# A two-layer diffusion step on one core: latent rows normalised, rotated and turned between the value and the query projections

## What is computed

```python
q_na, k_na, v_na, cq, ckv, k_rope = split(h @ w_in)         # 512, 512, 512, 256, 128, 32 columns
q_mla = (_rms_norm(cq, q_norm_g) @ w_uq).reshape(b, l, 8, 96)
ckv = _rms_norm(ckv, kv_norm_g)
k_rope = _axial_rope(k_rope, rows_pos, cols_pos)             # latent tokens only
kv = (ckv @ w_ukv).reshape(b, l, 8, 128)                     # keys and values of the latent heads
```

## Time and profile before

| | us |
|---|---|
| median of 3 runs | 1071.36 |
| lowest and highest | 1070.34, 1072.72 |
| profiled execution | 1072.17 |
| its span | 1070.3 |
| TensorE busy in it | 984.8 |

### The profile page before, as it was taken

The page is one execution under the profiler, slowest core; times in us unless marked ns, Lnnn a source line. Parts: engine busy times, 40 slices in busy tenths (PEclk is TensorE's granted clock), DMA queues, the critical chain, the costliest instruction groups (busy, mean ns, idle before and its releaser), DMA issues.

```text
span 1070.3 us, 14368 instructions
## 1 busy us (share of the span) xinstructions
PE 984.8 (92%) x5585; PEld 480.2 (45%) x5585; DVE 341.0 (32%) x872; ACT 251.6 (24%) x597; POOL 122.6 (11%) x138
## 2 busy tenths in 40 slices
PE   4899889999899999987889999999989999999896
PEld 3445546555433334432344554566553344343332
DVE  2200376521832122111330025764156112211226
ACT  2110155421411111111320103553041111111113
POOL 4120200000211111110022002000011111111103
PEclk8999999999899999999999999999998999999999
DMA  9952375378489999999995035662955999999993
GB/s 356 390 205 79 111 277 219 125 304 344 164 323 396 396 393 409 393 407 417 386 366 197 20 131 206 237 237 93 419 235 203 377 391 386 395 410 407 410 409 121
DMA packets 64666, 314.21 MB, mean 294 GB/s; under 512 B 7674, under 2 KB 9942, under 8 KB 38736
## 3 DMA queue, kind: packets, MB, share of 16 engines
q1 hardware_dynamic: 56112, 289.06, 69.2%
q0 software_dynamic: 7616, 21.01, 5.6%
q10 hardware_dynamic: 864, 3.15, 0.7%
HBM read 301.06 MB, written 17.53 MB: 298 GB/s over the span
## 4 chain that ended last, share of the span: by engine, by line
PE 71%; DMA 17%; DVE 6%; issue 2%; ACT 2%; SPq 2%; POOL 0%; DVEq 0%; ACTq 0%
PE psum L1066 15%; DMA arena<-in_w_up 12%; PE psum L1456 8%; PE psum L1310 8%; PE psum L1123 7%; DMA arena<-in_w_ada 5%; PE psum L1298 4%; PE psum L1289 3%; PE psum L983 3%; PE psum L1396 3%; PE psum L1426 2%; PE psum L1408 2%; PE psum L1078 2%; PE psum L1351 2%; PE psum L1022 1%
## 5 line engine op out<-in xcount | busy, mean ns | idle before, releaser
L1066 PE MATMUL psum<-arena 128*64 128x512 f32 x512 | 235.6, 608 | 21.7 <-DMA arena<-in_w_up 17.8
L1069 PE MATMUL psum<-arena 128*64 128x512 f32 x512 | 236.1, 609 | 0.0
L1066 PEld LDWEIGHTS psum<-arena 128*64 128x64 f32 x512 | 69.2, 140 | 168.6 <-issue 164.2
L1123 PE MATMUL psum<-arena 128*64 128x512 f32 x512 | 118.7, 600 | 3.3 <-ACT arena L1615 1.4
L2046 DVE SCALAR_TENSOR_TENSOR arena<-arena,psum 64x512 f32<-64x512 f32 (+1 forms) x32 | 23.9, 747 | 259.5 <-ACT arena L1609 259.5
L1456 PE MATMUL psum<-arena 128*128 128x384 f32 x256 | 86.7, 492 | 0.0
L1310 PE MATMUL psum<-arena 128*128 128x384 f32 x256 | 83.5, 487 | 1.2 <-PE psum L1310 0.6
L1609 ACT ACTIVATE arena<-psum 64x512 f32<-64x512 f32 (+1 forms) x32 | 20.6, 644 | 263.6 <-PE psum L1069 263.6
L1069 PEld LDWEIGHTS psum<-arena 128*64 128x64 f32 x512 | 69.2, 140 | 0.0
L1310 PEld LDWEIGHTS psum<-arena 128*128 128x128 f32 x256 | 48.3, 190 | 36.8 <-issue 4.0
L1456 PEld LDWEIGHTS psum<-arena 128*128 128x128 f32 x256 | 47.3, 190 | 32.4 <-issue 2.7
(11 more groups left out here) (305 smaller groups left out, 1216.5 us busy)
## 6 DMA issues: line engine op xcount, KB each, us to landing
arena<-in_w_gate SPq DMA_DIRECT2D x54, 1024.0 KB, 20.9
arena<-in_w_up SPq DMA_DIRECT2D x50, 1024.0 KB, 23.3
arena<-in_w_ada SPq DMA_DIRECT2D x24, 2048.0 KB, 7.8
arena<-in_w_down SPq DMA_DIRECT2D x48, 1024.0 KB, 22.8
arena<-in_w_down SPq DMA_DIRECT2D x32, 512.0 KB, 22.1
arena<-in_w_up SPq DMA_DIRECT2D x28, 512.0 KB, 21.2
arena<-in_w_in SPq DMA_DIRECT2D x6, 2048.0 KB, 14.6
arena<-in_w_gate SPq DMA_DIRECT2D x20, 512.0 KB, 14.5
```

What stands on the lines that cost most here:

```text
L1066: ins = nc.tensor.matmul(bank[b][0:MAIN, :], hg[:, k, 0:MAIN], row(wg[half], k), start=(k == 0), stop=(k == KD - 1))
L1069: ins = nc.tensor.matmul(bank[b][MAIN:P, :], hg[:, k, 0:MAIN], row(wu[half], k), start=(k == 0), stop=(k == KD - 1))
L1123: ins = nc.tensor.matmul(bank[6][MAIN * j:MAIN * j + MAIN, :], hidT[:, c, 0:MAIN], down_row(w[half], c)[:, 512 * j:512 * j + 512], start=( ...
```

## The change

The five groups of transposes that follow the keys are split. CQT, CKVT and KRT are filled between V and QK; KOUT and KC stay behind QK. The items are renumbered so that each keeps its engine: CQT 6 and 7, CKVT 8, KRT 9, QK 10 to 17, KOUT 18, KC 19. The wait for the caches moves from KC to CKVT, since `ckvn` holds cached rows too. ScalarE takes its statistics ahead of its V copy, VectorE its normalising and rotating ahead of its two V copies, and each then copies CQT, CKVT and KRT, then QK, KOUT, KC and QM items. No instruction is added or taken away, and no size changes. POOL's program is the same text, with KRT now coming earlier than KOUT by the whole QK projection.

```diff
--- before.py
+++ after.py
@@ -60,7 +60,7 @@
 ADA_EARLY = 4
 
 
-IT_REST, IT_V, IT_QK, IT_KOUT, IT_KC, IT_CQT, IT_CKVT, IT_KRT = 0, 3, 6, 14, 15, 16, 18, 19
+IT_REST, IT_V, IT_CQT, IT_CKVT, IT_KRT, IT_QK, IT_KOUT, IT_KC = 0, 3, 6, 8, 9, 10, 18, 19
 IT_QM, IT_VM, IT_KM, IT_QMT, ITEMS = 20, 26, 30, 38, 46
 UNITS = 24
 OUT_DMAS = 4
@@ -886,12 +886,16 @@
                     ins.then_inc(item_dve, 1)
 
         def copies_latent(eng, l, parity):
-            copy_out(eng, l, parity, IT_KOUT, IT_KC, lambda i: k_out)
-            copy_out(eng, l, parity, IT_KC, IT_CQT, lambda i: kcT.rearrange("p a b -> p (a b)"))
             copy_out(eng, l, parity, IT_CQT, IT_CKVT, lambda i: cqT[:, i, :], width=TOK,
                      scale=lambda i: vec[:, l, 64 + i:65 + i])
             copy_out(eng, l, parity, IT_CKVT, IT_KRT, lambda i: ckvT)
-            copy_out(eng, l, parity, IT_KRT, IT_QM, lambda i: krT[0:QKD, :], parts=QKD)
+            copy_out(eng, l, parity, IT_KRT, IT_QK, lambda i: krT[0:QKD, :], parts=QKD)
+
+        def copies_keys(eng, l, parity):
+            copy_out(eng, l, parity, IT_KOUT, IT_KC, lambda i: k_out)
+            copy_out(eng, l, parity, IT_KC, IT_QM, lambda i: kcT.rearrange("p a b -> p (a b)"))
+
+        def copies_queries(eng, l, parity):
             copy_out(eng, l, parity, IT_QM, IT_VM, lambda i: qtok[:, i // 2, 512 * (i % 2):512 + 256 * (i % 2)],
                      width=lambda i: 512 - 256 * (i % 2))
 
@@ -1298,7 +1302,23 @@
                         ins = nc.tensor.matmul(bank[(IT_V + t) % 4][:, :], hT[:, k, P * t:P * t + P], w[:, k, :],
                                                start=(k == 0), stop=(k == KD - 1))
                     ins.then_inc(item_ps, 1)
-                release(l, IT_QK)
+                release(l, IT_CQT)
+                pe.wait_ge(lora_norm, l + 1)
+                for i in range(2):
+                    item_free(pe, l, IT_CQT + i)
+                    for t in range(NT):
+                        ins = nc.tensor.transpose(bank[(IT_CQT + i) % 4][:, P * t:P * t + P], cqn[:, t, P * i:P * i + P], ident)
+                    ins.then_inc(item_ps, 1)
+                pe.wait_ge(cache_in, 64 * l + 64)
+                item_free(pe, l, IT_CKVT)
+                for m in range(4):
+                    ins = nc.tensor.transpose(bank[IT_CKVT % 4][:, P * m:P * m + P], ckvn[:, m, :], ident)
+                ins.then_inc(item_ps, 1)
+                pe.wait_ge(kr_ready, l + 1)
+                item_free(pe, l, IT_KRT)
+                for m in range(4):
+                    ins = nc.tensor.transpose(bank[IT_KRT % 4][0:QKD, P * m:P * m + P], kr[:, m, :], ident)
+                ins.then_inc(item_ps, 1)
                 for half in range(2):
                     key = ("q", l) if half == 0 else ("k", l)
                     loaded(key)
@@ -1319,24 +1339,8 @@
                     ins = nc.tensor.transpose(bank[IT_KOUT % 4][:, P * m:P * m + P], qkT[:, 4 + m, 0:P], ident)
                 ins.then_inc(item_ps, 1)
                 item_free(pe, l, IT_KC)
-                pe.wait_ge(cache_in, 64 * l + 64)
                 for m in range(4):
                     ins = nc.tensor.transpose(bank[IT_KC % 4][:, P * m:P * m + P], kc_tok[:, P * m:P * m + P], ident)
-                ins.then_inc(item_ps, 1)
-                pe.wait_ge(lora_norm, l + 1)
-                for i in range(2):
-                    item_free(pe, l, IT_CQT + i)
-                    for t in range(NT):
-                        ins = nc.tensor.transpose(bank[(IT_CQT + i) % 4][:, P * t:P * t + P], cqn[:, t, P * i:P * i + P], ident)
-                    ins.then_inc(item_ps, 1)
-                item_free(pe, l, IT_CKVT)
-                for m in range(4):
-                    ins = nc.tensor.transpose(bank[IT_CKVT % 4][:, P * m:P * m + P], ckvn[:, m, :], ident)
-                ins.then_inc(item_ps, 1)
-                pe.wait_ge(kr_ready, l + 1)
-                item_free(pe, l, IT_KRT)
-                for m in range(4):
-                    ins = nc.tensor.transpose(bank[IT_KRT % 4][0:QKD, P * m:P * m + P], kr[:, m, :], ident)
                 ins.then_inc(item_ps, 1)
                 item_wait(pe, l, IT_CQT)
                 item_wait(pe, l, IT_CQT + 1)
@@ -1672,7 +1676,6 @@
                     copy_rows(0, 0)
                 modulate(l, 0)
                 copy_out(act, l, 0, IT_REST, IT_V, lambda i: rest[:, i, :], width=REST)
-                copy_out(act, l, 0, IT_V, IT_QK, lambda i: vtok[:, i, :])
 
                 for t in range(NT):
                     item_wait(act, l, IT_REST + t)
@@ -1683,9 +1686,12 @@
                 st.sync()
                 nc.scalar.activation(rstat[:, 0:3], stat[:, 0:3], ACT.Sqrt, bias=eps, scale=1.0 / RANK_Q)
                 nc.scalar.activation(rstat[:, 3:6], stat[:, 3:6], ACT.Sqrt, bias=eps, scale=1.0 / RANK_KV).then_inc(lora_stat, 1)
+                copy_out(act, l, 0, IT_V, IT_CQT, lambda i: vtok[:, i, :])
                 load_table(ACT.Exp)
+                copies_latent(act, l, 0)
                 copies_qk(act, l, 0)
-                copies_latent(act, l, 0)
+                copies_keys(act, l, 0)
+                copies_queries(act, l, 0)
                 copies_values(act, l, 0)
                 copies_q(act, l, 0)
                 def exps(u):
@@ -2171,8 +2177,6 @@
                 else:
                     norm(2 * l)
                 copy_out(dve, l, 1, IT_REST, IT_V, lambda i: rest[:, i, :], width=REST)
-                copy_out(dve, l, 1, IT_V, IT_QK, lambda i: vtok[:, i, :])
-                copies_qk(dve, l, 1)
 
                 dve.wait_ge(lora_stat, l + 1)
                 st.did(v.reciprocal(rstat, rstat))
@@ -2190,7 +2194,11 @@
                 rope(kr[:, 3, HD:QKD].unsqueeze(1), 2, 1)
                 st.sync()
                 dve.sem_inc(kr_ready, 1)
+                copy_out(dve, l, 1, IT_V, IT_CQT, lambda i: vtok[:, i, :])
                 copies_latent(dve, l, 1)
+                copies_qk(dve, l, 1)
+                copies_keys(dve, l, 1)
+                copies_queries(dve, l, 1)
                 for t in range(1, NT):
                     item_wait(dve, l, IT_QM + 2 * t)
                     item_wait(dve, l, IT_QM + 2 * t + 1)
```

## The result

The changed kernel takes 1066.29 us in the median of 10 runs (1061.65 to 1068.77), the kernel before 1072.27 (10 runs, 1070.34 to 1075.47). The ratio is 0.9941, with a 95% interval of 0.9927 to 0.9956: 6.3 us less, between 4.7 and 7.8 (the two medians are 6.0 apart). The profiled execution of the changed kernel is its fastest, 1061.65.

What follows compares the result with a forecast made beforehand. TensorE holds 71% of the last-ending chain, DMA 17%, so TensorE's waits count. Gains of 3.11 and 4.85 sum to 7.96 us: 1064.2 from the profiled 1072.17, 1063.4 from the median, taken as 1064.0; range 1062.3 to 1067.8.

Steps and rivals of the forecast that it cites:

- Added ahead of the queries: Between values and queries, the transposes of `cqn`, `ckvn` and `kr` would add 1.66 us a layer to TensorE.
- Removed: Behind the keys, 4.77 us a layer would go: 5.24 between the starts of L1324 and L1351, less a pitch of 0.47.
- Net: In one layer's stretch from values to latent-head queries, 4.77 - 1.66 = 3.11 us gained.
- The clock, and layer 1: Behind layer 1's keys, half speed would vanish, worth 1.74 us, so layer 1 gains 3.11 + 1.74 = 4.85.
- The upper end: During the values, VectorE's normalising chain waits for all of POOL's bias addition and ends at 68.2, still 6.8 us early.
- The cover: Time between the normalising chain's end and the values' end on TensorE: 13.6 us, or 6.8 if POOL's addition holds the chain.
- The banks, the caches, the releases: Around the moved transposes, PSUM bank waits, cache transfers and SP's later release of `w_ada` pieces were taken to cost nothing.
- Passing on: Through the DMA-bound expert stages the gain reaches the end, since expert weights are issued earlier by the same amount.
- the new places: Rival: clock falls anyway at transposes ahead of queries or around the 0.70 us wait; 1066.0 or 1067.7 us; chance 0.16.
- Swallowing: Rival: expert-stage transfers absorb the gain, leaving 1071.4 us; chance 0.08 for all, 0.05 for half.
- The late chain: Rival: normalising ends beyond 78.1, so TensorE stands ahead of the queries; 1074.2 us if at 80 in both layers; chance 0.03.
- The sum: Over both layers, 3.11 + 4.85 = 7.96 us gained, giving a forecast of 1064.0 us.

Runs made afterwards that it cites:

- before_again: The kernel before, unchanged, profiled and timed again against itself: median 1072.47 us, ratio 0.9986 (0.9963 to 1.0009).
- single-layer kernels: The kernel before with VectorE's query and key copies put behind its normalising and rotating, in layer 0 alone or layer 1 alone: ratios 0.9952 and 0.9953.
- the two repeats: The changed kernel, unaltered, timed twice more against the kernel before: medians 1065.43 and 1065.86 us, ratios 0.9920 and 0.9924.
- after_again: The changed kernel, unaltered, run again beside the kernel before: median 1065.43 us, ratio 0.9920 (0.9893 to 0.9946).
- chain_behind_values: The changed kernel with value copies back ahead of ScalarE's statistics and VectorE's normalising chain: median 1073.84 us, ratio 1.0004 to the kernel before.

## Why the prediction was right, and where it was off

- *The terms of one layer.* Added ahead of the queries: 1.66 forecast, 1.56 measured. Removed: 4.77 forecast; 5.24 - 0.43 = 4.81 measured, and QM itself takes 8.21 from start to start instead of 8.29. From the first query product to KOUT it is 42.68 instead of 42.75. Net 3.40 in layer 0 against 3.11.
- *The clock, and layer 1.* 4.85 was forecast for layer 1 and 5.14 measured, but the split was wrong: the gaps were forecast at 3.11 and are worth 2.98, the fall at 1.74 and cost 2.15. The prediction gave layer 1 the gaps of layer 0 and took the difference of the two stretches, 58.49 - 56.75 = 1.74, for the price of half speed. The three other profiles of the kernel before have layer 1 without a fall, at 56.33 or 56.34. So its gaps alone are worth 56.34 - 53.36 = 2.98, 0.42 less than the 3.40 of layer 0, and the fall in it cost 58.49 - 56.34 = 2.15. The difference of 1.74 held both at once, which is why the sum does not show the error. The shorter gap comes from VectorE: in layer 0 of each of the four profiles it stands still for 0.56 us ahead of the rotations (L1855), in layer 1 it does not, and L1339 waits 1.44 instead of 1.85. The first line is layer 0 in the profile before, the second layer 1 of before_again:

```profile
120.24 0.40 DVE L1855 TENSOR_TENSOR arena<-arena 128x8 f32<-128x8 f32 x4 [0.56 <-DVE arena L2184]
645.91 0.61 PE L1339 MATMUL psum<-arena 128*96 128x128 f32 x4 [1.44 <-DVE arena L883]
```

  Why layer 0 has this pause is not shown. The step also took the fall for a feature of layer 1. It belongs to either layer, one of them in each profile of the kernel before, so the sum holds for an average execution; that one fall was the usual number, and not none or two, could not be known from one profile and is luck.
- *The chain under POOL's addition.* The upper end came true: 67.14, forecast 68.2 at most. What was held was a copy with one input, not the instructions with two that the prediction named (last section). The cover, 7.5 us in layer 0, sufficed.
- *The banks, the caches, the releases* cost nothing, as taken: no wait stands at CQT, CKVT, KRT or the first query group but the 0.30 that was there before.
- *Passing on.* Shown by the single-layer kernels and by the constant length of what follows. The first expert weights were issued at 216.32; 217 had been forecast.
- *The rivals.* No fall came in the new places. Swallowing is refuted. The late chain is real as a mechanism, at 4.08 us a layer when the cover is taken away, but does not arise.
- *The sum.* 7.96 us forecast. By the traces the two stretches together went from 115.0 to 115.2 down to 106.7, 8.2 to 8.5 us. The first timed comparison gave 6.3 (4.7 to 7.8), the two repeats 8.6 and 8.1. The local sum lies within the intervals of the repeats and just outside the first. The medians are closer together, 6.0, 6.9 and 7.3 us apart, all below the local sum. And beside the same runs that gave the 8.6, the unchanged kernel came out at 0.9986, 1.5 us less than itself, so part of the 8.6 may be scatter. The timed runs put the gain between 6 and 8.6 us; the forecast of 1064.0 was 2.3 us below the first median, 1066.29. Whether the local sum reaches the end whole is not settled, and what the first set lacks, up to 2 us, is not explained. Other falls of the clock move such a sum: at the REST projection one came in 6 of 8 layers of the profiles of the kernel before and in 4 of 6 of the changed one, at 1.5 to 1.7 us each, and the profiled execution of 1061.65 has none. Why they come in one execution and not in another stays open.

## What to carry to other kernels

When the engine on the critical path waits for a short chain of small operations elsewhere, see when the inputs of that chain were ready. Here they had been ready for 46 us and the chain stood behind copies in its own queue; moving one line of that queue gave as much as the whole rearrangement. A pause in a thin stretch of TensorE may cost more than its own length, so price it at both clock levels, and look at several profiles before putting a fall down to one place.

## What was not expected of the hardware

A VectorE copy of 32 columns, 0.17 to 0.18 us in the kernel before, was recorded with 6.69 us when POOL's addition had begun 0.01 us earlier. Layer 1 of the same profile, first in VectorE's timeline, then in POOL's:

```profile
572.26 4.67 DVE L2186 COPY arena<-arena 128x32 f32<-128x32 f32 x1
```

```profile
570.22 6.67 POOL L754 TENSOR_TENSOR arena<-arena 128x3072 f32<-128x3072 f32 x1 [11.29 <-DMA arena<-bias_padded]
```

In all six layers of the three profiles the copy ended within 0.05 us of the end of POOL's addition (63.47 and 63.43, 576.93 and 576.89 in those shown; 65.04 and 65.00 in layer 0 of after_again), whatever it had left, and POOL's addition kept its 6.67 us. The reciprocal of 6 columns just ahead of it was not held: 0.19 in after_again at 58.67, when the addition had been running since 58.33. The Trainium skill (SBUF — State Buffer, section "SBUF: two separate sides") has the exclusive port pair for this; it names VectorE instructions in a two-port mode beside those with two SBUF inputs, and the copy, with a single input, would be of the first kind. The prediction had looked only at instructions with two inputs; here all of these ran behind the addition, so no run shows whether they would be held. A value copy out of PSUM in the middle of an addition was not held: 0.69 at 60.98 in the kernel before, with the addition from 57.06 to 63.73. Where the chain runs behind the addition, in chain_behind_values, the first 32-column copy took 0.18 again (at 77.28). What was not tried is the changed kernel without POOL's addition, so the cause is read from the coinciding ends and this comparison, and not from an edit made for it.

The clock fell to 1.2 GHz behind the keys after two pauses of 0.70 and 1.00 us with eight transposes between them, during the six transposes that follow (in before_again at about 121.5, ahead of the gap at L1339), and in other executions stayed at 2.4 GHz through the same work and a further pause of 1.44 to 1.85. With three dummy products in the gaps it stayed up in both layers.
